# The low parts of the input chunks moved from GpSimd to VectorE, with a reordered layer boundary

## The reference, cut to what matters

```python
def modulate_pre(x, g_pre, shift, scale):
    return rms_norm(x, g_pre) * (1.0 + scale[:, None, :]) + shift[:, None, :]
def gated_post_add(x, y, g_post, gate, weight):
    return x + weight * gate[:, None, :] * rms_norm(y, g_post)
def swiglu_ffn(h, w_in, w_out):
    g, u = jnp.split(h @ w_in, 2, axis=-1)
    return (jax.nn.silu(g) * u) @ w_out
...
        h = modulate(rmsnorm(x, norm1_g[i]), sh1, sc1)
        hc = modulate(rmsnorm(xc, norm1_g[i]), csh1, csc1)
...
        x = x + g1 * y
        x = x + g2 * swiglu(modulate(rmsnorm(x, norm2_g[i]), sh2, sc2), ffn_w_gu[i], ffn_w_down[i])
```

## Time and profile before

| | |
|---|---|
| median of three runs | 2540.94 us (2533.14 to 2543.69) |
| the profiled execution | 2539.34 us |
| its span | 2537.6 us |
| mean granted TensorE clock | 0.930 |
| TensorE busy | 2251.8 us, 89% |
| VectorE busy | 1190.5 us, 47% |
| ScalarE busy | 960.4 us, 38% |
| GpSimd busy | 104.9 us, 4% |
| DMA | 411.40 MB, mean 162 GB/s |

### The profile page before, as it was taken

How to read it: one execution, slowest core, us unless ns; L and a number is a source line. 1 busy time by engine, 2 the same in 40 slices (tenths; PEclk the granted TensorE clock), 3 DMA queues, 4 the chain that set the end, 5 groups by cost and what they waited for, 6 DMA issues and landing times.

```text
span 2537.6 us, 35245 instructions
## 1 busy us (share of the span) xinstructions
PE 2251.8 (89%) x14142; PEld 1882.8 (74%) x14142; DVE 1190.5 (47%) x1907; ACT 960.4 (38%) x1522; POOL 104.9 (4%) x221
## 2 busy tenths in 40 slices
PE   4899798899789997767899879878999999797998
PEld 1798686798688976534897779656777767686997
DVE  0444554444543445554544565684322233565444
ACT  0433522433433335444433533563312122355343
POOL 1100100000110001000000200000100000201000
PEclk7899898899879998778999989989999999899999
DMA  7786485686348763101776333102444342221653
GB/s 280 266 276 245 151 298 215 231 277 241 123 162 285 257 250 119 50 1 67 248 266 249 103 89 100 34 1 75 165 159 149 117 149 99 59 84 51 199 182 116
DMA packets 243820, 411.40 MB, mean 162 GB/s; under 512 B 8173, under 2 KB 188870, under 8 KB 243686
## 3 DMA queue, kind: packets, MB, share of 16 engines
q1 hardware_dynamic: 243206, 408.49, 46.3%
q0 software_dynamic: 480, 1.05, 0.5%
HBM read 408.47 MB, written 1.05 MB: 161 GB/s over the span
## 4 chain that ended last, share of the span: by engine, by line
PE 76%; DVE 10%; ACT 6%; DMA 5%; issue 3%; POOL 1%; SPq 0%; ACTq 0%; DVEq 0%; POOLq 0%
PE bank L1527 19%; PE bank L1476 13%; PE bank L1477 12%; PE bank L1478 12%; PE bank L1451 4%; PE bank L1580 2%; PE bank L1582 2%; PE bank L1581 2%; DMA stage<-in_ffn_w_out 2%; ACT gate_b L775 1%; ACT w_hi L608 1%; DMA ada<-in_ada_w 1%; DVE w_lo L961 1%; PE bank L1672 1%; PE bank L1614 1%
## 5 line engine op out<-in xcount | busy, mean ns | idle before, releaser
L961 DVE TENSOR_TENSOR w_lo<-stage,w_hi 128x2048 fp32r<-128x2048 f32 x255 | 585.6, 2298 | 736.5 <-ACT w_hi L608 736.5
L1476 PE MATMUL bank<-h_hi,w_hi 128*128 128x256 f32 (+1 forms) x2432 | 741.9, 305 | 9.1 <-POOL h_lo L568 6.7
L608 ACT CAST w_hi<-stage 128x2048 fp32r<-128x2048 f32 x255 | 484.5, 1902 | 674.6 <-PE bank L1478 255.1
L1477 PE MATMUL bank<-h_lo,w_hi 128*128 128x256 f32 (+1 forms) x2432 | 732.8, 301 | 0.0
L1478 PE MATMUL bank<-h_hi,w_lo 128*128 128x256 f32 (+1 forms) x2432 | 732.4, 301 | 0.0
L1476 PEld LDWEIGHTS bank<-h_hi,w_hi 128*128 128x128 f32 x2432 | 472.4, 194 | 70.7 <-issue 55.9
L1477 PEld LDWEIGHTS bank<-h_lo,w_hi 128*128 128x128 f32 x2432 | 472.4, 194 | 14.9 <-issue 1.2
L1478 PEld LDWEIGHTS bank<-h_hi,w_lo 128*128 128x128 f32 x2432 | 472.0, 194 | 14.1
L1527 PE MATMUL bank<-w_hi,h_hi 128*128 128x512 f32 x776 | 252.7, 403 | 38.7 <-DVE h_lo L970 36.6
L1527 PE MATMUL bank<-w_hi,h_lo 128*128 128x512 f32 x776 | 248.0, 397 | 0.0
L1527 PE MATMUL bank<-w_lo,h_hi 128*128 128x512 f32 x776 | 247.8, 397 | 0.0
(11 more groups left out here) (194 smaller groups left out, 2022.4 us busy)
## 6 DMA issues: line engine op xcount, KB each, us to landing
ada<-in_ada_w SPq DMA_DIRECT2D x120, 1024.0 KB, 7.0
stage<-in_ffn_w_in SPq DMA_DIRECT2D x88, 1024.0 KB, 6.4
stage<-in_ffn_w_out SPq DMA_DIRECT2D x44, 1024.0 KB, 5.0
stage<-in_ffn_w_gu SPq DMA_DIRECT2D x44, 1024.0 KB, 5.1
stage<-in_ffn_w_down SPq DMA_DIRECT2D x22, 1024.0 KB, 4.9
stage<-in_a_w_in SPq DMA_DIRECT2D x12, 1024.0 KB, 7.7
stage<-in_diff_w_in SPq DMA_DIRECT2D x12, 1024.0 KB, 5.2
ada<-in_kv_ada_w SPq DMA_DIRECT2D x8, 1024.0 KB, 8.6
```

Of the source, the lines that this page charges most:

```text
L608: a.copy(w_hi[:, s, :], stage[:, s, :]).then_inc(hi_done, 1)
L961: v.tensor_tensor(w_lo[:, s, :], stage[:, s, :], w_hi[:, s, :].bitcast(F32), ALU.subtract).then_inc(lo_done, 1)
L1476: m.matmul(dst[:, 0:T], wh, h_hi[:, h0:h0 + T], start=(k == ks[0]), stop=False)
L1477: m.matmul(dst[:, 0:T], wh, h_lo[:, h0:h0 + T], start=False, stop=False)
```

## The change

1. GpSimd's `lo` goes to VectorE. At T = 256 the low parts follow the affines two chunks behind; at T = 512 those of the first pair of tiles stand ahead of the last tile's norm, the second pair's behind its affines. GpSimd has only start-up work left.
2. Projections down stagger their last two units, not three.
3. Behind each unit `mid_split` of the next comes before `split` of the unit two ahead.
4. `split` of the next layer's first unit stands at the beginning of the boundary.
5. At T = 256 (but layers 3 and 4) the transposes write banks 0 to 3; so the first half vector of layers 1, 2 and 6 goes ahead of the last transposes.
6. The gate matmuls of layers 5 and 9 run after the second unit of the projection down (in banks 0 and 1), with the first `mid_split` earlier; in layer 7 one gate goes ahead of the ot transposes, one behind them.
7. Table loads are issued by SyncE, ahead of layer 7's or 9's own weight loads, once the last gate matmul of the layer before has run.
8. The tables of q take 10 operations, made before the first unit's rope, and those of k 10, made after it (`make_tables`).

```diff
+            def load_tables(s):
+
+                w = Wide(s)
+                prev = subs[s["n"] - 1]
+                sp.wait_ge(pe_s, t.at((f"s{prev['n']}", "gate", prev["Td"] // 256 - 1, 1)))
+                for k in range(2):
+                    sp.dma_start(flat_diag[:, k * 256:k * 256 + 2 * w.dh].rearrange("p (t d) -> p t d", t=2),
+                                 w.rope[k].rearrange("(t p) d -> p t d", p=P)).then_inc(tables_landed, 16)
+                for k in range(2):
+                    src = io[w.norms[k]][0].partition_broadcast(P).unsqueeze(1).broadcast_to([P, w.hh, w.dh])
+                    sp.dma_start(flat_diag[:, 512 + k * 256:768 + k * 256].rearrange("p (h d) -> p h d", d=w.dh),
+                                 src).then_inc(tables_landed, 16)
+                if w.diff:
+                    for k, name in enumerate(("q1", "k1", "q2", "k2")):
+                        sp.dma_start(lam_in[:, k, :], io[f"diff_lambda_{name}_2"][0].partition_broadcast(P)).then_inc(lam_landed, 16)
...
+                    if s["kind"] in ("diff", "gqa"):
+                        load_tables(s)
...
-            def lo(s, k, tt):
-                tag = f"s{s['n']}"
...
-                t.done(g.tensor_tensor(dst, src, hi, ALU.subtract), pool_s, (tag, "lo", k, tt))
-
-            for s in subs:
-                if s["T"] == 256:
-                    for tt in range(2):
-                        for k in range(KC):
-                            lo(s, k, tt)
-                else:
-                    for c in s["cs"]:
-                        for k in s["ks"]:
-                            lo(s, k, c)
-                if s["kind"] in ("diff", "gqa"):
-                    w = Wide(s)
-                    pool.wait_ge(dve_s, t.at(x_mark(s["n"], 1)))
...
                     table(ACT.Sqrt)
+                    split(nu)
...
-                    if s and tt == n_prev - 2:
-                        if s["T"] == 512 and n_prev == 2:
-                            for k in s["ks"][0:5]:
-                                hi_pair(s, k, s["cs"][0])
-                        split(nu)
...
+                def turn_over(j, i):
+
+                    if i is not None or j + 1 < s["bsteps"]:
+                        mid_split(s, j + 1, i)
+                    if i is not None or j + AHEAD < s["bsteps"]:
+                        split(s["u"] + s["units"] + j + AHEAD, i, RING)
+                    if j == 0 and i is None and s["kind"] in ("nsa", "gqa"):
+                        gate(s, tag, 0)
+                for_b(act, s, turn_over)
...
+            def affines(s, tt, src_tag):
+
+                for n, k in enumerate(s["ks"]):
+                    affine(s, k, tt, src_tag)
+                    if n >= 2:
+                        lo(s, s["ks"][n - 2], tt)
+                for k in s["ks"][6:]:
+                    lo(s, k, tt)
+
+            def affine_pairs(s, ks, c, with_lo=True):
+
+                for n, k in enumerate(ks):
+                    affine_pair(s, k, c)
+                    if n >= 2 and with_lo:
+                        lo(s, ks[n - 2], c)
+                if with_lo:
+                    for k in ks[-2:]:
+                        lo(s, k, c)
...
+                if s and n_prev:
+                    split(nu)
...
                     y_update(prev, tt)
+                    if s and s["T"] == 512 and tt == n_prev - 1:
+                        for k in s["ks"]:
+                            lo(s, k, s["cs"][0])
                     if s and tt in tiles:
                         x_norm(s, tt)
                     if s and s["T"] == 256 and tt in tiles:
-                        for k in s["ks"]:
-                            affine(s, k, tt, f"s{s['n']}")
+                        affines(s, tt, f"s{s['n']}")
...
+                            affine_pairs(s, s["ks"], s["cs"][0], False)
                         if n_prev == 4 and tt in (1, 2):
-                            for k in s["ks"][4 * tt - 4:4 * tt]:
-                                affine_pair(s, k, s["cs"][0])
-                    if s and tt == n_prev - 2:
-                        split(nu)
+                            affine_pairs(s, s["ks"][4 * tt - 4:4 * tt], s["cs"][0], False)
                 if s and s["T"] == 512:
-                    for k in s["ks"]:
-                        affine_pair(s, k, s["cs"][1])
+                    affine_pairs(s, s["ks"], s["cs"][1])
...
+                def make_tables(k):
+
...
+                        for a_ in range(2):
                             for part in range(2):
+                                o = a_ * 2 * q4 + part * q4
+                                out_ = sg[:, tt * 256:(tt + 1) * 256].rearrange("p (h d) -> p h d", h=hh)[:, :, o:o + q4]
+                                sin = flat_diag[:, 256 + tt * dh + o:256 + tt * dh + o + q4].unsqueeze(1).broadcast_to([P, hh, q4])
+                                g0 = a_ * 2 * q4 + (1 - part) * q4
+                                gg = gain[:, g0:g0 + q4].unsqueeze(1).broadcast_to([P, hh, q4])
                                 ins = v.tensor_tensor(out_, sin, gg, ALU.mult)
-                t.done(ins, dve_s, (tag, "tables"))
+                    t.done(ins, dve_s, (tag, "tables", k))
+
+                make_tables(0)
...
+                        if n == 0:
+                            make_tables(1)
...
+                        if s["kind"] == "diff" and j == 0 and tt == 1:
+                            pe.wait_ge(act_s, t.at((tag, "gateb", 1, 1)))
...
+                step(1, None)
+                if s["kind"] in ("nsa", "gqa"):
+                    gate(s, tag, 0)
                 if nb == FC // 2:
-                    step(1, None)
                     with pe.Fori(1, 3) as i:
                         for j in range(RING):
                             step(j - 1, i)
+                    step(nb - 3, None)
                 for tt in range(n_tiles):
-                    for j in range(nb - 3, nb):
+                    for j in range(nb - 2, nb):
...
+                    pe.wait_ge(act_s, t.at((tag, "evO", 7)))
+                    gate(s, tag, 0)
...
                     t.marks[("ada", "free")] = t.now["pe_s"]
+                    gate(s, tag, 1)
...
+            def fills(s):
+                return s is not None and s["n"] > 0 and s["nvec"] > 0 and s["xb"] == 0
...
+                if fills(nxt):
+                    vec_acc(nxt["v"], 0)
```

More of the change, by code:

```diff
@@ L942, in _ @@
                     wide_act(s, tag)
[L943 to L947 removed]
+                if s["kind"] in ("ffn", "conv"):
+                    for k in range(s["Td"] // 256):
+                        gate(s, tag, k)
+                    if T == 512:
+                        mid_split(s, 0)
+                def turn_over(j, i):
[6 more added lines that the diff above has]
+                for_b(act, s, turn_over)
             boundary(subs[-1], None)
@@ new lines, in gate @@
+            def gate(s, tag, st):
+                if st == 0:
+                    dve.wait_ge(ada_col, rv(s["v0"] + 2) + 1)
+                gv = modv[:, s["v0"] + 2, 8 * st:8 * st + 8]
+                if s["post"]:
+                    t.done(v.scalar_tensor_tensor(out=modc[:, 2, 8 * st:8 * st + 8], in0=gv, scalar=s["weight"],
+                                                  in1=cols[:, s["g_post"]:s["g_post"] + 8], op0=ALU.mult, op1=ALU.mult), dve_s, (tag, "G", st))
+                    gv = modc[:, 2, 8 * st:8 * st + 8]
+                    dve.wait_ge(dve_s, t.at((tag, "G", st)))
+                for h in range(2):
+                    if st:
+                        dve.wait_ge(pe_s, t.at((tag, "gate", st - 1, h)))
+                    for k in range(4):
+                        ins = v.tensor_scalar(diag[:, h, k * P:(k + 1) * P], ident[:, :], gv[:, 4 * h + k:4 * h + k + 1], None, ALU.mult)
+                    t.done(ins, dve_s, (tag, "diag", st, h))
@@ L1121, in kv_dve @@
                     if n < 2 and s["n"] + 1 < len(subs):
-                        for k in range(KC):
-                            affine(subs[s["n"] + 1], k, n, tag)
+                        affines(subs[s["n"] + 1], n, tag)
                     if n < 2:
@@ L1829, in block3 @@
                             up_step(j, i, 2, (0, 2), first,
-                                    {(0, 0): (lambda: vec_acc(s["v"], 0),)} if first and s["nvec"] else None)
+                                    {(0, 0): (lambda: vec_acc(s["v"], 0),)} if first and s["nvec"] and not fills(s) else None)
                         if s["nvec"]:
@@ L1842, in _ @@
                     if early:
-                        also[1, 0] = (lambda: gates(s, tag),)
+                        also[1, 0] = (lambda: gate(s, tag, 0),)
                     up_step(10, None, 2, (0, 2), False, also)
@@ L1864, in _ @@
                     wide_pe(s, tag)
-                if not early:
-                    gates(s, tag)
+                if s["kind"] in ("ffn", "conv") and not early:
+                    for k in range(s["Td"] // 256):
```

(1 more changed line is left out.)

168 lines of the change are left out of this document (78 added, 90 removed).

## The result

The changed kernel takes 2482.05 us, the median of four runs (2479.7 to 2484.1), against 2542.3 us for the kernel before on the same chip: a ratio of 0.977, 95% interval 0.974 to 0.980. The forecast was 2481 us. The profiled executions are 2539.3 and 2484.1 us, and their spans differ by 55.2 us, against 58.3 in the sum (the medians differ by 60.3). That close agreement hides terms that were wrong in both directions, so the work of this part is to take the sum apart.

A forecast was written before the change was run, and what follows sets the result against it. TensorE was taken as the bound, so only its stands were priced: 26 + 13.6 + 10.2 + 10.3 + 24.9 - 4.0 - 0.7 - 18.0 - 4 = +58.3, 2539.3 to 2481 us. Own range 2462 to 2500, overall 2448 to 2518.

The forecast's parts named there:

- The low part of mid first, and the clock behind it: Down-projections: mid's low part ahead of the weights' ends TensorE's h_lo stands (+26) and half clock after them (+13.6).
- Boundaries at T = 256: Between layers: +10 in all, of which 0.7 at each of five (3.5), 2.2 behind layer 9, half vectors 4.5.
- Half vectors: In three boundaries half an ada vector moves from behind the first transposes into the wait: 1.5 each, +4.5 us.
- Gates: Layers 5, 7 and 9: gate work moved into TensorE's stands hides there, 2.1, 6.1 and 2.1 us: +10.3.
- Tables: Layers 7 and 9: earlier loads and fewer operations before the first rope save 16.2 and 8.7 us: +24.9.
- Low parts on VectorE: Costs VectorE time: kv (layer 3) -4.0, layer 0's start -0.7, three T=512 boundaries -18.0, half clock there -4.
- The context tiles' norms behind the split: Boundary 6 to 7: these norms wait behind the weight split (1.90 + 2.29 and handoffs), -4.6 us.
- B: Rival: the clock stays low, new stands of 1.5 to 1.9 us bringing half-clock windows; about 2504 us, chance 0.16.
- C: Rival: mid's low parts stay late in the staggered units, so 24 + 13.6 go; about 2518 us, chance 0.08.
- D: Rival: table loads come late or push the units, a stand remaining in each attention layer; about 2506 us, chance 0.05.
- E: Rival: low parts break VectorE's run, a step taking about 1.1 us instead of 0.58; about 2561 us, chance 0.05.
- F: Rival: weight loads take over, TensorE running into them when the stands go; about 2510 us, chance 0.05.

The follow-up runs named there:

- e12_midfirst: The kernel before with one part of the change alone, mid's low part ahead of the weights' behind each unit: 2507.3 us against 2541.15.
- e1_order: The changed kernel with the weights' split again ahead of the split of mid behind each unit of a projection down: 2493.7 us.
- e11_split: The changed kernel with the next layer's first weight split back between the two tiles, in boundaries into layers at T = 256: 2505.6 us.
- e2_three: The changed kernel with three staggered units again in the projections down of layers 0, 2, 4 and 10: 2496.7 us.
- e9_nofill: The changed kernel with the first half vector of layers 1, 2 and 6 behind their first products again: 2489.1 us.
- e13_gate59: e8_best with ScalarE's gate copies in layers 5 and 9 one place later, behind the split of mid's next chunk: 2443.4 us.
- e4_tables: The changed kernel with rope table and lambda vector loads issued by GpSimd again, the fewer and deferred table operations kept: 2482.06 us.
- e5_queue: The changed kernel with low parts and table loads both on GpSimd, the loads behind the low parts: 2486.5 us.
- e10_gates7: The changed kernel with both gates of layer 7 behind the ot transposes again, the first split of mid still early: 2489.6 us.
- e6_kv: The changed kernel with VectorE's copies of the second unit's keys ahead of the second tile's affines and low parts in layer 3: 2482.05 us.
- e8_best: e3_pool with context tiles' norms ahead of the weight split (6 to 7), and three staggered units with the split's old place in layers 7 and 8: 2449.0 us.
- e3_pool: The changed kernel with the low parts of the input chunks back on GpSimd, all other parts kept: 2464.2 us.

## Why the prediction was right, and where it was not

**The low part of mid first, and the clock behind it (26 + 13.6).** Right in mechanism, 34 instead of 39.6 for the order alone (e12_midfirst). Not seen was that the rest of the change, with two staggered units, would have done nearly the same for the long projections (e1_order).

**Boundaries at T = 256 (3.5 of the 10.2).** Right in place and size: 10.15 us for the forecast 10.1. Of the 3.5 by which the table's 24.0 passes the 20.5, 2.0 are layer 1's, whose projection down ran its first 3.8 us at half clock before (414.20 to 417.99) and does not now. What carries it is the early split (e11_split: 23.6 us), which in turn needs the two staggered units (e2_three: 14.6 us). The prediction summed both as 0.7 a boundary because it set them against the third unit's cover; undone alone, each is dear.

**Half vectors (4.5).** Mis-sized: 7.0. The prediction read the 2.15 us of the earlier trace rows as half clock and put full clock at about 1.1. At 1.00 it takes 1.92 (e9_nofill), so the term should have been near 2 each; the 1.3 us of vector loads in layer 1 was not forecast.

**Gates (10.3).** In layer 7 about as forecast: 6.1, against 7.15 by stage and 4.35 when undone (7.6 by the medians). In layers 5 and 9 the step "gate work moved into such places hides there" failed: the 2.0 us stands moved behind the gate matmuls. The prediction did not ask what is queued behind the copies on ScalarE (e13_gate59 shows it).

**Tables (24.9).** The sum was right (15.4 and 8.8 by stage, 22.6 less 7.15 of gates and the 8.8 saved up to layer 9's first rope), the cause half named. "GpSimd issues these loads late" was true because its low parts stood ahead of them, and so the change has two cures for it, of which each is enough (e4_tables, e5_queue).

**Low parts on VectorE (-26.7 with the T = 512 boundaries).** The sign was right. In layer 3 the term was mis-sized, -8.8 for -4.0 (-5.8 in other profiles of the same code): 16 pairs put the copies later, where a stand of 0.70 became stands of 1.52 and 4.15, 5.0 us in all. The rest is half clock behind the second (0.50 for 6.8 us from 690.6; 3.4 us in e10_gates7 and e11_split) and later in the layer. e6_kv shows that a weight split is late next. At T = 512 the low parts cost little (under 0.5 a tail); the stands of 1.58 and 1.57 were forecast at 1.9 each, and are gone in e8_best with the third unit and the split's old place. The context tiles' norms behind the split were forecast at 4.6 and the exchange gave 7.5.

**The rivals.** B in part: a 3.41 us half-clock window is gone from behind all eight stands, and the new stands of 1.31 to 1.58 us brought none; those of 2.0 us that moved behind the gates of layers 5 and 9 did, though the stands of 2.0 us ahead of these gates had brought none before. C, D, E and F did not happen. The prediction weighed a rule of the Trainium skill, Perfetto Trace Analysis, "Optimizing Scalar/DVE Operations": where VectorE is saturated, handing work to ScalarE or even GpSimd may make sense. The runs agree with it: the low parts on GpSimd are 17.8 us faster (e3_pool), half of it in layer 3 by these profiles and the rest in the boundaries, those of T = 256 too, which the prediction had left out of the rule. VectorE is busy for only 49% of the changed kernel's span, so what counts is whether it is saturated in such a stretch.

That the time came out within about 1 us of the forecast is partly luck. In the profiles 6 us more in half vectors and boundaries stand against 5 less in layer 3 and 7 less in layers 5 and 9; the spans fall short of the sum by 3 us and the medians pass it by 2.

## What to carry to other kernels

A change made of many parts can pay for a part that loses: measure each alone, undone from the whole, before the whole is kept. Where an engine has spare time at another's expense, look not only at the length of the moved work but at what stands behind it in both lists: the table loads behind GpSimd's low parts, the cast behind ScalarE's gate copies. Two parts that cure the same stand can be worth little when one is undone (the table loads' place: nothing; the order behind each unit: 11.7 us) and much when one is done alone (the order: 33.8 us), so both directions have to be run.

## What was not expected

A part of the difference between single stages is the clock. Layer 8's gates took 6.7 us in the profiles of the changed kernel, e6_kv, e10_gates7 and e11_split, 5.4 in e4_tables and e5_queue, and 4.1 in those of the kernel before and the seven other experiments, with the same code. And the start of layer 0's projection down came 1.7 us earlier in e8_best than in e13_gate59, whose matmuls reached full clock at 79.1 and 81.4 us. (The profile of e8_best shows 1.00 for the time before 79.1 as well, but its matmuls of 128x256 take 0.41 us there and 0.28 afterwards, as those of e13_gate59 do at 0.50 and at 1.00.) No run here shows what decides it.
